# A hybrid decoder layer: the vector constants first in their queue, longer idle products, and a router with its weights stationary

## The reference

```python
def rms_norm(x, g):
    var = jnp.mean(xf * xf, axis=-1, keepdims=True)
    return (xf * lax.rsqrt(var + EPS)).astype(x.dtype) * g

xn = rms_norm(h, norm_mix_g[l])          # (272, 1024), the head of the kernel
proj = xn @ w_in[l]
...
h = h + merged @ w_out[l]                # (256, 1024) from here on
xt = rms_norm(h, norm_ffn_g[l])
logits = xt @ w_router + b_router        # (256, 1024) @ (1024, 32)
top_val, top_idx = lax.top_k(logits, 4)
gates = softmax(top_val)
for e in range(32):                      # tokens of expert e, at most 64 in one pass
    hdn = xt[tokens] @ w_up[e] + b_up[e]
    act = min(glu, 7) * sigmoid(1.702 * glu) * (clip(lin, -7, 7) + 1)
    y[tokens] += gate * (act @ w_down[e] + b_down[e])
out = rms_norm(h + y, norm_final_g)[16:]
```

## Time and profile before

| | us |
|---|---|
| median of 3 runs | 1226.03 (1224.76 to 1226.2) |
| the profiled execution, its own time | 1225.45 |
| its span in the trace | 1223.4 |
| TensorE busy | 1163.6 (95% of the span) |
| VectorE busy | 311.5 (25%) |
| ScalarE busy | 200.4 (16%) |
| mean granted TensorE clock | 0.993 of full |

### The profile page before, as it was taken

How to read it: one execution, slowest core, us unless ns; L and a number is a source line. 1 busy time by engine, 2 the same in 40 slices (tenths; PEclk the granted TensorE clock), 3 DMA queues, 4 the chain that set the end, 5 groups by cost and what they waited for, 6 DMA issues and landing times.

```text
span 1223.4 us, 14042 instructions
## 1 busy us (share of the span) xinstructions
PE 1163.6 (95%) x5656; PEld 538.4 (44%) x5656; DVE 311.5 (25%) x617; ACT 200.4 (16%) x408; POOL 5.4 (0%) x13
## 2 busy tenths in 40 slices
PE   8999999999999999999999999999999999999996
PEld 6767788856333333333333333333333333333332
DVE  3555530114122221212122212222121212221213
ACT  2257720102011110100011111000101100010002
POOL 0000001000000000000000000000000000000000
PEclk9999999998999999999999999999999999999999
DMA  9733325434999999999999999999999999999994
GB/s 379 313 145 136 143 102 185 163 111 169 421 426 427 429 429 428 429 429 428 429 429 429 429 429 429 429 429 429 429 429 429 429 429 429 429 428 429 429 428 189
DMA packets 34906, 441.93 MB, mean 361 GB/s; under 512 B 4080, under 2 KB 4096, under 8 KB 6592
## 3 DMA queue, kind: packets, MB, share of 16 engines
q1 hardware_dynamic: 33696, 438.61, 85.6%
q0 software_dynamic: 608, 1.86, 0.5%
q10 hardware_dynamic: 576, 1.11, 0.2%
HBM read 440.52 MB, written 1.05 MB: 361 GB/s over the span
## 4 chain that ended last, share of the span: by engine, by line
PE 65%; DMA 32%; DVE 1%; ACT 1%; issue 0%; ACTq 0%; SPq 0%; DVEq 0%
DMA ring<-in_w_exp_dram 31%; PE ps L834 21%; PE ps L865 12%; PE ps L495 9%; PE ps L784 4%; PE ps L798 4%; PE ps L681 2%; PE ps L744 2%; PE ps L764 2%; PE ps L705 1%; PE ps L851 1%; PE ps L625 1%; PE ps L565 1%; PE ps L531 1%; PE ps L790 1%; DMA vec<-in_vec_dram 1%
## 5 line engine op out<-in xcount | busy, mean ns | idle before, releaser
L834 PE MATMUL ps<-ring,work 128*64 128x512 f32 x2048 | 461.7, 596 | 42.5 <-DMA ring<-in_w_exp_dram 42.5
L834 PEld LDWEIGHTS ps<-ring,work 128*64 128x64 f32 x2048 | 141.3, 137 | 353.0 <-issue 264.0
L865 PE MATMUL ps<-ring,work 128*64 128x512 f32 x1024 | 226.8, 595 | 0.0
L1439 DVE TENSOR_TENSOR X<-ps,X 128x1024 f32<-128x1024 f32 x64 | 78.4, 1225 | 369.2 <-PE ps L798 369.2
L495 PE MATMUL ps<-work,ring 128*128 128x256 f32 (+2 forms) x576 | 130.7, 384 | 0.0
L865 PEld LDWEIGHTS ps<-ring,work 128*64 128x64 f32 x1024 | 70.8, 137 | 133.2 <-issue 133.2
L495 PEld LDWEIGHTS ps<-work,ring 128*128 128x128 f32 (+1 forms) x576 | 106.7, 188 | 18.9 <-issue 1.4
L1453 DVE TENSOR_SCALAR work<-ps 128x512 f32<-128x512 f32 x32 | 22.1, 691 | 347.4 <-PE ps L834 347.4
L1060 ACT ACTIVATE work<-work 128x512 f32<-128x512 f32 x32 | 20.2, 630 | 524.1 <-DVE work L1453 524.1
L784 PEld LDWEIGHTS ps<-work 128*128 128x128 f32 x544 | 65.5, 197 | 26.4 <-issue 26.4
L798 PE MATMUL ps<-work 64*128 64x512 f32 x256 | 72.3, 641 | 0.0
(11 more groups left out here) (221 smaller groups left out, 580.4 us busy)
## 6 DMA issues: line engine op xcount, KB each, us to landing
ring<-in_w_exp_dram SPq DMA_DIRECT2D x192, 2048.0 KB, 33.0
ring<-in_w_mix_dram SPq DMA_DIRECT2D x29, 1024.0 KB, 7.0
ring<-in_w_mix_dram SPq DMA_DIRECT2D x2, 576.0 KB, 19.0
X<-in_x_dram SPq DMA_DIRECT2D x2, 512.0 KB, 18.4
ring<-in_w_mix_dram SPq DMA_DIRECT2D x4, 256.0 KB, 20.1
out_dram<-X SPq DMA_DIRECT2D x2, 512.0 KB, 2.6
ring<-in_w_mix_dram SPq DMA_DIRECT2D x1, 640.0 KB, 11.3
work<-in_xT_dram ACTq DMA_DIRECT2D x2, 272.0 KB, 4.4
```

The lines of the kernel that those rows point to most:

```text
L834: ins = nc.tensor.matmul(ps[CAP * c:CAP * c + CAP, b, :], xeT[:, u // 2, k, CAP * (u % 2):CAP * (u % 2) + CAP], ring[:, s + k % SPAN, 512 ...
L865: ins = nc.tensor.matmul(ps[CAP * c:CAP * c + CAP, 5, :], actT[:, j, CAP * g:CAP * g + CAP], wv[:, k, 512 * c:512 * c + 512], start=(f == ...
L1439: V.tensor_tensor(xi, ps[:, 6:8, :], xi, ALU.add).then_inc(scat_added, 1)
```

## The change

Three parts. In ScalarE's list the load of `vec` stands first, ahead of the two chunks of `xT`, and the load of `ca` moves behind the two squares. Products whose result nobody reads (`keep_clock_long`, 256 or 272 moving columns) are put into the waits: three ahead of the wait for the reciprocal, one behind the product that spreads it, one ahead of the wait for the logits of tile 1, and one behind `up_bias` in place of the four of 128 columns. The router keeps the 32 columns of weights stationary, a quarter of the k-tiles in each of four column groups with 128 token columns moving; VectorE copies the four partial sums out of PSUM (`part`), and one more product with the 0/1 matrix `pick` (`fold`) adds the four groups up and turns the result back to tokens x experts.

```diff
-    b[:2 * E, slice(*CB["pick"])] = (n[None, :] % E == np.arange(2 * E)[:, None] % E)
+    b[:, slice(*CB["pick"])] = (n[None, :] % E == np.arange(P)[:, None] % E)
...
+            def keep_clock_long(bank, cols, n):
+                for _ in range(n):
+                    nc.tensor.matmul(ps[:, bank, 0:cols.shape[1]], ones, cols, start=True, stop=True)
...
             ins.then_inc(xsum_done, 1)
+            keep_clock_long(2, xsq[:, 0, :], 3)
             pe.wait_ge(rstd_ready, 1)
...
             ins.then_inc(rstd_done, 1)
+            keep_clock_long(2, xsq[:, 0, :], 1)
...
-                    ins = nc.tensor.matmul(ps[:, i, 0:E], hT[:, i, k, :], wr[:, k, :], start=(k == 0), stop=(k == KT - 1))
-                ins.then_inc(logits_done, 1)
+                    q = k % 4
+                    ins = nc.tensor.matmul(ps[E * q:E * q + E, i, 0:P], wr[:, k, :], hT[:, i, k, :], start=(k < 4), stop=(k >= 4))
+                ins.then_inc(part_done, 1)
+
+            def fold(i):
+                pe.wait_ge(part_ready, i + 1)
+                nc.tensor.matmul(ps[:, i, 2 * P:2 * P + E], part[:, i, :], pick_e[:, 0:E], start=True, stop=True)\
+                  .then_inc(logits_done, 1)
...
             router(0)
             turn_h(1)
+            fold(0)
             router(1)
+            fold(1)
...
             pe.wait_ge(sel0_ready, 1)
+            pe.wait_ge(xn2_ready, 1)
+            keep_clock_long(7, xn2[:, 0, 0:256], 1)
             pe.wait_ge(logits_read, 1)
             up_bias(0)
-            keep_clock(7, 4)
+            keep_clock_long(7, xn2[:, 0, 0:256], 1)
             pe.wait_ge(mask_ready, 1)
...
         def _(act):
+            act.dma_start(vec[:, :], vec_in[:, :]).then_inc(vec_in_s, 16)
             for c in (1, 3):
                 act.dma_start(xT[:, 2 * c:2 * c + 2, :], xT_in[:, 2 * c:2 * c + 2, :]).then_inc(xT_in_s[c], 16)
-            act.dma_start(vec[:, :], vec_in[:, :]).then_inc(vec_in_s, 16)
-            act.dma_start(ca[:, P:], ca_in[:, P:]).then_inc(const_in, 16)
...
                 nc.scalar.activation(xsq[:, 2 * c:2 * c + 2, :], xT[:, 2 * c:2 * c + 2, :], ACT.Square).then_inc(xsq_act, 1)
+            act.dma_start(ca[:, P:], ca_in[:, P:]).then_inc(const_in, 16)
             act.wait_ge(xsum_done, 1)
...
-                link(V.scalar_tensor_tensor(out=lg[:, i, :], in0=ps[:, i, 0:E], scalar=rs2[:, i:i + 1], in1=brt,
+                link(V.scalar_tensor_tensor(out=lg[:, i, :], in0=ps[:, i, 2 * P:2 * P + E], scalar=rs2[:, i:i + 1], in1=brt,
...
                 V.tensor_copy(hT[:, i, 4:8, :], ps[:, 5 + 2 * i, :].rearrange("p (k t) -> p k t", k=4))\
                  .then_inc(hT_ready2, 1)
+                dve.wait_ge(part_done, i + 1)
+                V.tensor_copy(part[:, i, :], ps[:, i, 0:P]).then_inc(part_ready, 1)
                 if i == 1:
                     logits(0)
```

More of the change, by code:

```diff
@@ L247, in layer @@
         y = view(512)
+        part = view(TT * P).rearrange("p (i t) -> p i t", i=TT)
         assert at[0] <= gel_at
@@ L318, in layer @@
             sem(n) for n in ("xsq_act", "xsq_dve", "xsum_done", "xstd_done", "xn_ready"))
+        part_done, part_ready = (
+            sem(n) for n in ("part_done", "part_ready"))
         rstd_ready, rstd_done, sel0_ready, logits_read = (
```

## The result

The changed kernel took 1229.6 us (median of 7, 1227.61 to 1232.06) against 1225.14 (7, 1224.68 to 1226.38): ratio 1.0036, interval 1.0024 to 1.0048. It is slower, by about 4.5 us. The profiled execution took 1228.9, its span is 1227.1, 3.7 us longer than before's.

A forecast was written before the change was run, and what follows sets the result against it. TensorE was taken to bound the kernel ahead of the experts and full DMA engines within them. Head +1.2 and router stretch +1.4 gave +2.6 on 1226.03, so 1228.6 us, range 1223.5 to 1230.8.

The forecast's parts named there:

- The bound: Whole kernel: TensorE bounds ahead of the experts, full DMA engines in them; a shift at the experts' start reaches the end.
- Part 1, turns: Head: queues advance by turns, so chunk 3 lands last instead of the constants; reciprocal at 11.1, not 9.39, +1.7 us.
- Part 2, idle products: Head: idle products delay the spreading product but may save 1.5 us in the first projection; with the queue, +1.2 us.
- two cases: Head, queue and idle products together: clock kept, +0.5 us; clock fallen, about +2 us; the middle, +1.2, was taken.
- Part 3, the router: Router to gather: router saves 1.2 us each, but VectorE's early copy delays tile 1; +1.4 us with the clock fallen.
- rival B: Around tile 1's logits: idle products and faster router hold the clock, -1.7 us there; ends about 1225, chance 0.15.
- the sign that I had set: Output projection's end to first expert product: forecast wrong if under 18.0 us; also wrong if the reciprocal begins before 9.4.
- The sum: Whole kernel: +1.2 for the head and +1.4 for the router stretch make +2.6 us, forecast 1228.6.
- Rival E: Both waits: the clock falls before the idle products, which run at half; +2.7 and +2.2 us, 1231, chance 0.12.
- Rivals C and D: Head: engines pass whole loads, chunk 3 little late, 1225.1, chance 0.13; the second adds rival B, 1222.0, chance 0.10.

The follow-up runs named there:

- padded: The changed kernel with only five products added in TensorE's branch for overfull experts, which does not run: 1230.29 us, ratio to before 1.0037.
- the weights held: The changed kernel with SyncE's first weight load held until chunk 3 of xT has landed: 1229.52 us, ratio to before 1.0026.
- the router with late copies: Kernel before with new router, fold and late copies, no long idle products, constants behind both chunks, eight products that do not run: 1223.56 us, ratio 0.9982.
- both orders undone: Changed kernel, constants behind both xT chunks, partial-sum copies after tile 1's X additions (tile 0) and tile 0's logits (tile 1): 1220.83 us; with non-running products 1220.32.
- the copy late: The changed kernel with VectorE's copy of tile 0's partial sums behind the two additions of tile 1 to X: 1226.35 us, ratio to before 1.0002.

## Why the prediction was right, by its steps

**The bound.** Right. The start of the experts moved by 2.07 us and the start of the last down projection by 3.03; in ten of the twelve experiments, and before, the stretch between is 908.3 to 908.8 whatever its start. In the changed kernel it was 909.46; that 1 us is in no step of mine, and its cause is open.

**Part 1, turns.** Right: the last of the three loads lands last, and it was chunk 3. I put its squaring at 9.39 and the reciprocal at 11.1; they came at 9.96 and 11.89 in the profile. The 1.7 us for the way from squaring to reciprocal were 1.9. The load of `ca` was worth nothing, as said: with it in its old place the router of tile 0 started at 276.67, behind the squares at 276.43 to 276.84. In the runs with this order the squaring began at 8.79, 9.61, 9.96 and 11.85, while with the chunks first it lay between 5.95 and 6.57: the last packets are exposed to more chance than I allowed.

**Part 2, idle products.** I had two cases, +0.5 with the clock kept and about +2 with it fallen, and took 1.2. The clock fell, at 7.9 us, ahead of the idle products and not within them, and stayed down to 14.7. They took 3.09 us, the 2.9 of the estimate at half clock, which I had used only as a bound. The head cost 2.87 in the profile: +2.50 at the reciprocal, +1.97 from there to the first projection (14.37 - 11.89 and 15.66 - 14.37, against 0.64 and 1.16), and -1.68 in the first projection, which met the full clock again (together 2.79). It cost about the same where the constants stood first on the old kernel (281.60 - 278.25 = 3.4, another execution). The term was mis-sized by taking the middle of two cases, and neither is what happened: the clock fell and was back ahead of the first projection. My ground for the second case was the length of the wait, over 3 us against the 2.74 of the old kernel. The traces don't bear it out as the cause: in the changed kernel the clock fell 1.0 us into the wait, in the old kernel at 11.34, 1.3 us after the wait had ended. What the idle products are worth with the old order, -1.4 at the router (276.84 against 278.25), was near the -1.5 of the sum; over all traces with the chunks first they start it at 275.40 to 276.84, those without at 278.25 to 279.56.

**Part 3, the router.** The router took 0.65 us (0.7 predicted), VectorE reached X at 283.42 - 281.12 = 2.3 behind the router's start (2.55), the turning began 3.0 behind it (3.35), and the logits of tile 1 were read 7.62 behind it, against 7.1 in the sum. The position products came 0.28 us behind the start of the mask's last instruction. So the step stood. Its outcome has two forms. With the clock fallen to the end of gather the middle took 19.50, 19.53 and 19.59 in three traces, +1.5 to +1.6, where I had +1.4; in the profile of the changed kernel the clock came back at 287.8 and it took 17.19, -0.8 where rival B had -1.7. By the sign that I had set, a middle shorter than 18.0 us, the forecast was wrong for this execution and right for the same middle in the three other traces. The seven timed executions divide in a like way: three with a mean granted clock of 0.993, the profiled one among them, took 1227.61 to 1229.45, the four with 0.990 or 0.991 took 1229.6 to 1232.06. B was not the rule, but something near it is the profile shown.

**The sum** of 2.6 against 4.5 measured: the head was 1.7 short in the profile, the tail, which I didn't look at, 0.3 to 1.7 in the runs where the stall is seen. For the changed kernel the times don't confirm that last part: padded it was not faster. That the forecast came as near as it did to the 3.7 us of the profile is in part luck: a middle 2.2 below its term hid a head 1.7 above it, and the 0.96 of the expert stage and the 0.67 of the tail are in no term.

**Rival E** had the mechanism that most executions seem to have shown. In the changed kernel with the padding the clock fell ahead of the idle products in both waits (at 7.95 and at 284.4), and they ran at half, as E says. Head and middle then cost +1.97 and +1.60 against before, where E had +2.7 and +2.2.

**Rivals C and D** fell: a load does not pass in one turn. By the sentence of the Trainium skill ("DMA: Bandwidth & Descriptors", Queues, rings and completion order) that an engine drains a packet of 9 to 17 descriptors before it switches, chunk 3 would have been late by little, as rival C says. No trace here agrees: beside the weights it was squared at 8.79 to 11.85, and near 6.1 only with the weights held.

## What to carry to other kernels

Moving a small load to the front of a queue doesn't make the last load land earlier; it exchanges which one is last. Ask which of the loads has the longest way to go after it lands, and put that one first. An instruction that waits for another engine belongs in an in-order list behind everything that the other engine will need next: the same copy, four instructions later, made the middle 14.05 us and not 17.19 to 19.6. And a loss can hide good parts: the idle products alone won 4.3 us, the router with late copies 2.0, all of it with both orders undone 5.2 to 5.7, and as combined in the change they lost 4.5.

## What the runs showed of the hardware

- The place of TensorE's code matters. Five never executed products ahead of the last ones made TensorE stop for 1.11 us within them, and the same five removed a stop of 1.16 us in another program. TensorE's unpadded list of the changed kernel stopped after three entries in all six of its traces (for 0.50 to 1.32 us), and in none of three with five products more. The point of the stop moved with the code: after three entries in the changed kernel, which has four products more than before, after one entry with five more. That TensorE waits there for a piece of its code fits these moves and the 16 KB packet of the queue `instruction`, 1.26 to 1.53 us after whose end it goes on in all seven traces; the traces don't name the engine that the packet is for. The tail was 14.34 us in all seven traces without the stop and 14.68 to 16.00 in the seven with it. Where the granted clock fell about the end of the stop (three traces), the five entries behind it took 2.41 to 2.92 us and not 1.55.
- The same TensorE work met a different clock from one execution to the next: the middle of the changed kernel took 17.19 us in one and, with nothing else than code that does not run added, 19.59 in another. Three of the fourteen traces kept the clock through the middle, all three with the late copy; three others with the late copy lost it for 3.4 to 6.8 us. What decides it is open.
- Chunk 3 against the weights: in the run with the copy late it was squared only at 11.85. There all but the last four of its 128 packets of data had ended by 9.65, and the four ended at 9.99, 10.38, 10.77 and 11.16. Steps of 0.39 us are about an 8 KB packet (0.31) and a 2 KB packet (0.09) in turn, as if one DMA engine were behind the others. Why it was is open.
